# Norm means kept as columns of tokens, and the state-space scan taken in turn with the projections

## The reference

```python
def rms_norm(x, g):
    y = x32 * lax.rsqrt(jnp.mean(x32 * x32, axis=-1, keepdims=True) + RMS_EPS)
    return y * g

# first_block, DEPTH = 2
for l in range(DEPTH):
    u = rms_norm(h, ln_mix[l])
    (aq, ak, av, bq, bk, bv, cq, ck, cv, dq, dzf, dzb, di, dg, gz) = split_in(u @ w_in[l])
    # y_a windowed attention, y_b rope attention, y_c differential attention, y_d gated linear attention
    merged = sum(gate[:, :, n] * (y_n @ w_branch[l, n]))
    h = h + merged @ w_out[l]
    u = rms_norm(h, ln_ffn[l])
    h = h + (silu(u @ w_ffn_gate[l]) * (u @ w_ffn_up[l])) @ w_ffn_down[l]
x = rms_norm(h, ln_final)[:, META_END:]

# second_block: shift, scale and gate come from a conditioning vector
x = x + gate0 * rms_norm(swiglu(modulate(rms_norm(x, pre1), ...)), post1)
h = modulate(rms_norm(x, premix), shift, scale)
q, k, v, u = split(h @ w_in2)                  # 512, 128, 128 and 512 columns
attn = sliding_window_attention(q, k, v, sinks)
ssm = s5_ssm(u, ...)                           # y = Re(C x) + D u, x a diagonal complex recurrence; GELU, GLU
y = concat(rms_norm(attn, n_attn), rms_norm(ssm, n_ssm)) @ w_out2
x = x + gate1 * rms_norm(y, postmix)
x = x + gate2 * rms_norm(swiglu(modulate(rms_norm(x, pre2), ...)), post2)
```

## Time and profile before

| | us |
|---|---|
| median of 3 runs (lowest to highest) | 3252.58 (3252.03 to 3252.73) |
| profiled execution | 3256.16 |
| its span | 3253.3 |
| mean granted TensorE clock over the span | 0.964 of full |

### The profile page before, as it was taken

The page is one execution under the profiler, slowest core; times in us unless marked ns, Lnnn a source line. Parts: engine busy times, 40 slices in busy tenths (PEclk is TensorE's granted clock), DMA queues, the critical chain, the costliest instruction groups (busy, mean ns, idle before and its releaser), DMA issues.

```text
span 3253.3 us, 51837 instructions
## 1 busy us (share of the span) xinstructions
PE 3037.7 (93%) x21724; PEld 2591.9 (80%) x21724; DVE 1775.1 (55%) x3325; ACT 1011.7 (31%) x1740; POOL 220.4 (7%) x455
## 2 busy tenths in 40 slices
PE   7989999999999899999999999989999797789997
PEld 7767998999999887789897888858888364568886
DVE  4564577457556447457745757556356344553334
ACT  4655232232122246523223222242222114332221
POOL 0130221000000101122200000000000000000000
PEclk8999999999999999999999999989999898999999
DMA  5201111135433320112123545212234200113231
GB/s 176 99 15 46 58 59 57 70 131 175 150 134 111 119 78 27 46 50 66 58 71 141 180 146 178 100 53 104 101 126 162 91 34 12 66 65 105 84 103 70
DMA packets 74495, 302.48 MB, mean 93 GB/s; under 512 B 10728, under 2 KB 11112, under 8 KB 69272
## 3 DMA queue, kind: packets, MB, share of 16 engines
q1 hardware_dynamic: 57880, 230.04, 20.8%
q0 software_dynamic: 16384, 69.13, 5.8%
HBM read 288.51 MB, written 14.63 MB: 93 GB/s over the span
## 4 chain that ended last, share of the span: by engine, by line
PE 83%; DVE 9%; ACT 5%; issue 2%; POOL 0%; DMA 0%; DVEq 0%; ACTq 0%; SPq 0%
PE acc L1047 18%; PE acc L1048 17%; PE acc L1049 17%; PE acc L1309 5%; PE acc L1310 5%; PE acc L1311 5%; PE acc L1081 3%; ACT temps L1690 2%; PE acc L1212 2%; DVE work L1999 1%; PE acc L1066 1%; PE acc L1354 1%; PE acc L1186 1%; DVE normed L2017 1%; PE acc L1375 1%
## 5 line engine op out<-in xcount | busy, mean ns | idle before, releaser
L1048 PE MATMUL acc<-normed_r,toep_r 128*128 128x512 f32 (+1 forms) x1824 | 643.7, 353 | 0.0
L1619 ACT ACTIVATE toep_r<-ring 128x1024 fp32r<-128x1024 f32 (+2 forms) x340 | 392.7, 1157 | 711.4 <-PE acc L1049 710.6
L2050 DVE TENSOR_TENSOR ring_r<-ring,toep_r 128x1024 fp32r<-128x1024 f32 (+2 forms) x340 | 458.1, 1348 | 263.6 <-ACT toep_r L1619 263.3
L1048 PEld LDWEIGHTS acc<-normed_r,toep_r 128*128 128x128 f32 x1824 | 345.3, 189 | 46.3 <-issue 0.2
L1047 PE MATMUL acc<-work_r,toep_r 128*128 128x512 f32 (+1 forms) x1024 | 354.7, 346 | 6.5 <-DVE temps_r L2041 6.3
L1049 PE MATMUL acc<-work_r,ring_r 128*128 128x512 f32 (+1 forms) x1024 | 353.6, 345 | 0.0
L1047 PE MATMUL acc<-mixed_r,toep_r 128*128 128x264 f32 (+1 forms) x1056 | 344.1, 326 | 5.1 <-DVE ring_r L2050 4.4
L1049 PE MATMUL acc<-mixed_r,ring_r 128*128 128x264 f32 (+1 forms) x1056 | 340.0, 322 | 0.0
L1047 PE MATMUL acc<-temps_r,toep_r 128*128 128x512 f32 x768 | 304.5, 396 | 24.6 <-DVE normed_r L2036 15.2
L1048 PE MATMUL acc<-work_r,toep_r 128*128 128x512 f32 (+1 forms) x880 | 307.3, 349 | 0.0
L1309 PE MATMUL acc<-residual_r,toep_r 128*128 128x264 f32 (+1 forms) x1024 | 302.1, 295 | 1.6 <-DVE mixed L2237 1.6
(11 more groups left out here) (394 smaller groups left out, 5362.8 us busy)
## 6 DMA issues: line engine op xcount, KB each, us to landing
ring<-in_w_pair SPq DMA_DIRECT2D x176, 512.0 KB, 3.5
ring<-in_w_down SPq DMA_DIRECT2D x64, 704.0 KB, 4.1
ring<-in_w_gb SPq DMA_DIRECT2D x64, 640.0 KB, 3.9
extra<-in_w_ada POOLq DMA_DIRECT2D x18, 1024.0 KB, 6.4
toep<-in_w_ada POOLq DMA_DIRECT2D x18, 1024.0 KB, 5.9
ring<-in_w_tm SPq DMA_DIRECT2D x24, 512.0 KB, 4.5
ring<-in_w_out SPq DMA_DIRECT2D x24, 512.0 KB, 3.5
ring<-in_w_fm SPq DMA_DIRECT2D x20, 512.0 KB, 3.9
```

The costliest lines, as they stand in the source:

```text
L1048: mm(out, wh, xl[:, a:z], start=False, stop=False)
L1619: A(high(ld), slot(ld), ACT.Copy).then_inc(S["w_high"], 1)
L2050: V.tensor_tensor(low(ld), slot(ld), high(ld), ALU.subtract).then_inc(S["w_low"], 1)
```

## The change

The mean stands in columns of tokens. `mean_tile` takes the squares as stationary operand, 128 tokens (or 88, for 528) at a time, and one constant column as moving operand; each matmul leaves 128 tokens' partial sums in one column of bank 6. DVE sums the columns of all tiles (a tensor_reduce), ACT roots 128x4 (or 88x6), DVE inverts as much, and a new `spread_root` on TensorE multiplies each column, broadcast as stationary operand, by the identity, which puts the result of all tokens into all partitions of bank 7 (or 6 and 7). DVE's norm instructions read it from there. In the scaled FFN norms ACT copies it to `RINV`, and the spread stands behind u0. `sqrt_table` is a root of one column, put ahead of places where roots follow, so that the table is loaded there: at the start, ahead of the second half's down jobs of every FFN, ahead of the out jobs of both layers, and ahead of n_attn's squares. An Exp moves behind pre1's squares.

Behind premix ACT adds the shift, tile by tile, and TensorE waits per tile. The u jobs come first (and their loads); q, k and v go one by one, through bank 7, between the scan's parts. Some scratch tiles move to other buffers, since U now stays in use.

```diff
@@ norm(): where the mean and the root stand
-                     acc=PS[:, 6:6 + len(pieces), 0:pieces[0][1] - pieces[0][0]],
+                     rows=88 if len(pieces) == 2 else P, count=6 if len(pieces) == 2 else 4,
+                     r=PS[:, 6:8, 64:328] if len(pieces) == 2 else PS[:, 7:8, :],
@@ TensorE, mean_tile and spread_root
-                for s, (a, z) in enumerate(n["pieces"]):
-                    last = mm(n["acc"][:, s, :], mean[P * len(n["tiles"])], x[:, a:z],
-                              start=i == 0, stop=i == len(n["tiles"]) - 1)
+                a, at = n["pieces"][0][0], n["count"] * (min(i, 1) if n["total"] is not None else i)
+                for t in range(n["count"]):
+                    last = mm(PS[0:n["rows"], 6, at + t:at + t + 1], x[:, a + n["rows"] * t:a + n["rows"] * (t + 1)],
+                              mean[P * len(n["tiles"])][:, 0:1], start=True, stop=True, skip_group_check=True)
                 last.then_inc(S["sq_used"], 1)
+            def spread_root(n):
+                if n["n"]:
+                    wait(pe, norms[n["n"] - 1]["done"][-1])
+                pe.wait_ge(S["mean_inverted"], n["n"] + 1)
+                rows, each_piece = n["rows"], n["count"] // len(n["pieces"])
+                for t in range(n["count"]):
+                    a = rows * (t % each_piece)
+                    last = mm(n["r"][:, t // each_piece, a:a + rows], n["stat"][:, t:t + 1].to_broadcast([rows, P]),
+                              ident[0:rows, 0:rows], start=True, stop=True, skip_group_check=True)
+                last.then_inc(S["mean_spread"], 1)
@@ TensorE, ffn
                         split_lin(u)
+                        if i == 0 and f["scaled"]:
+                            spread_root(f["norm"])
@@ TensorE, second_block (every other norm: spread_root behind its mean_square)
                 mean_square(b2["premix"])
-                wait(pe, b2["premix"]["done"][-1])
-                for j in b2["q"] + b2["k"] + b2["v"] + b2["u"]:
-                    lin(j)
+                spread_root(b2["premix"])
+                for i, j in enumerate(b2["u"]):
+                    lin(j, [(S["u_shifted"], k + 1) for k in range(KT)] if i == 0 else ())
@@ TensorE, state_space (projection(i): the matmuls of q, k or v number i)
                 local_states(0)
+                projection(0)
                 lag_kernels()
+                local_states(1)
+                projection(1)
                 for q in range(4):
-                    if q < 3:
-                        local_states(q + 1)
-                    outputs(q)
+                    if q == 3:
+                        projection(5)
+                    outputs(q)
+                    if q < 2:
+                        local_states(q + 2)
+                    if q < 3:
+                        projection(q + 2)
@@ ACT, root, ffn, second_block
-                A(two(RINV, n["pieces"]), n["acc"], ACT.Sqrt, bias=epsc).then_inc(S["mean_read"], 1)
+                act.wait_ge(S["mean_summed"], n["n"] + 1)
+                A(n["stat"], n["stat"], ACT.Sqrt, bias=epsc[0:n["rows"], :]).then_inc(S["mean_rooted"], 1)
...
                     root(f["norm"])
+                    act.wait_ge(S["mean_spread"], f["norm"]["n"] + 1)
+                    A(two(RINV, f["pieces"]), f["norm"]["r"], ACT.Copy).then_inc(S["rinv_ready"], 1)
...
+                for k in range(KT):
+                    wait(act, b2["premix"]["done"][k])
+                    x = U[:, k, META:L]
+                    A(x, x, ACT.Identity, bias=mod[:, 24 + k:25 + k]).then_inc(S["u_shifted"], 1)
@@ DVE, rinv
-                V.reciprocal(r, r).then_inc(S["rinv_ready"], 1)
+                V.tensor_reduce(n["stat"], PS[0:n["rows"], 6, 0:k * n["count"]].rearrange("p (i t) -> p t i", i=k), AX, ALU.add
+                                ).then_inc(S["mean_summed"], 1)
+                dve.wait_ge(S["mean_rooted"], n["n"] + 1)
+                V.reciprocal(n["stat"], n["stat"]).then_inc(S["mean_inverted"], 1)
```

More of the change, by code:

```diff
@@ L319, in build @@
         ostat = cell(20)
+        meanstat, rootc = [cell(6) for _ in range(2)], cell(1)
         dec = [cell(2) for _ in range(2)]
@@ L428, in build @@
         KD = lambda q, lag: span(X, KD0 + 512 * q + P * lag, P)
-        MP = [span(Ut, 512 * k, 512) for k in range(4)]
-        WS, ZS = pair_of(Ut, 2048), pair_of(Ut, 3072)
+        MP = [span(X, xa + 512 * k, 512) for k in range(4)]
+        WS, ZS = pair_of(toep, 4096), pair_of(X, xa + 2048)
         ZO = [pair_of(E, 1536), pair_of(Yt, 4 * L)]
@@ L670, in build @@
         b2["premix"] = norm(H, b2["post1"]["done"], range(KT), TOKENS)
[L671 to L681, removed]
         b2["u"] = []
@@ L686, in build @@
             j.freed = mark("fm_ready")
+        b2["qkv"] = [load(ins["w_in2"][i], KT, cols=P) for i in range(6)]
+        for i, ld in enumerate(b2["qkv"]):
+            ld.done = (S["proj_full"], i + 1)
         b2["glu"] = []
@@ L1500, in second_block @@
                 mean_square(b2["pre1"])
+                spread_root(b2["pre1"])
                 ffn(b2["ffn1"], ssm=True)
@@ L1515, in second_block @@
                 mean_square(b2["n_attn"])
+                spread_root(b2["n_attn"])
                 mean_square(b2["n_ssm"])
+                spread_root(b2["n_ssm"])
                 for i, j in enumerate(b2["out"]):
@@ L1519, in second_block, with projection @@
                 mean_square(b2["postmix"])
+                spread_root(b2["postmix"])
                 mean_square(b2["pre2"])
+                spread_root(b2["pre2"])
                 ffn(b2["ffn2"])
                 mean_square(b2["post2"])
+                spread_root(b2["post2"])
+            def projection(i):
+                ld = b2["qkv"][i]
+                pe.wait_ge(w_ready[ld.slot], 16 * (ld.turn + 1))
+                if i:
+                    pe.wait_ge(S["proj_read"], i)
+                for t in range(4 if i == 5 else 1):
+                    for k in range(KT):
+                        if i == 5:
+                            a = META + P * t
+                            last = mm(PS[:, 7, P * t:P * t + P], U[:, k, a:a + P], slot(ld)[:, k, :], start=k == 0,
+                                      stop=k == KT - 1)
+                        else:
+                            last = mm(PS[:, 7, :], slot(ld)[:, k, :], U[:, k, META:L], start=k == 0, stop=k == KT - 1)
+                last.then_inc(S["proj_full"], 1)
             def state_space():
@@ L1680, in ffn @@
                         advance(u.loads[0])
+                    if half:
+                        sqrt_table()
                     for i, j in enumerate(f["down"][half]):
@@ L1970, in first_block @@
                     high_weights(j.loads[0])
+                sqrt_table()
                 squares(b2["n_attn"])
-                squares(b2["n_ssm"], b2["n_attn"]["done"][-1])
+                squares(b2["n_ssm"])
                 high_tiles(b2["x_out"])
@@ L2761, in first_block @@
                 added(b2["post1"], fg(1))
-                normed(b2["premix"], fg(2), U, shift(3))
+                normed(b2["premix"], fg(2), U)
                 state_space()
```

71 lines of the change are left out of this document (47 added, 24 removed).

## The result

The changed kernel takes 3261.77 us (median of 14 runs, 3257.66 to 3266.42) against 3254.54 (14 runs, 3252.03 to 3257.94) for the kernel before: ratio 1.002, 95% interval 1.0012 to 1.0028. It is slightly slower, where 3240 was forecast.

A forecast was written before the change was run, and what follows sets the result against it. TensorE's work plus its waits, for norm reciprocals and behind premix, was taken to bound the kernel. Norm gains and losses, +8.0 in the FFN and -20.5 in the scan summed to -12.5: 3240 us, range 3206 to 3251.

The forecast's parts named there:

- The small chain and its norms: In every norm, small sum, root, reciprocal and spread take 1.85 us warm or 2.8 cold; post1 took 5.42 before.
- The half-clock mean tile: In norms at half clock, a mean tile's eight records cost 1.71 us, above the pace at which squares arrive.
- the burst at 578.70: 20 narrow records after idle took 3.75 us, against 2.02 at 325.58; read as narrow matmuls not raising the clock.
- rival (a): Narrow matmuls in the norms run at full clock, mean tiles cost 0.87: -45.2 us, 3207; chance 0.18.
- The FFN norms: In the two scaled FFN norms, silu waits for the spread and an uncovered table load: +4.0 us each.
- The mixer: Premix's first use to first score: per-tile shift, u first, projections inside the scan; 110.9 us against 131.4, -20.5.
- Rival (b): The six projections inside the scan run at half clock: +41.4 us there, 3281 in all; chance 0.06.
- the sum: Terms of the edited places, from norms to scan, added to -12.5 us for the whole kernel.
- the forecast has 0.64: Chance given to the main forecast for the whole kernel, with its own range 3231 to 3246.
- the four norms behind dense work: post1, final, postmix and post2 start at high clock and take 3.3 us for 5.42: -2.1 each, -8.4.
- the prediction's cold start of the projections: At the u jobs behind premix, some 2.2 us lost, half of the 4 us until full pace.
- Rival (c): No change: squares loaded as weights cost up to 0.25 us a record, 2.0 a tile: 3253; chance 0.12.

The follow-up runs named there:

- e5: Changed kernel with wide mean tiles, root and reciprocal back in the two scaled FFN norms, early loads ahead of both layers' out jobs removed; 3247.07 us, ratio 0.9978.
- e2: Changed kernel with all thirteen norms put back to wide and all early table loads removed, keeping the mixer's new order; 3236.21 us, ratio 0.9935.
- e3: Changed kernel with eight norms wide again; columns stay in ly1.norm, final, post1, postmix and post2; 3231.10 us, ratio 0.9922.
- e9: e3's kernel with ly1.norm wide as well, columns left in final, post1, postmix and post2 alone; 3233.64 us, ratio 0.993.
- e7: Changed kernel plus two wide fp32 matmuls, results unused, ahead of the second model's attention; 3252.29 us, ratio 0.9995.
- e12 to e15: Changed kernel plus one, three, four and again two unused wide matmuls ahead of the second model's attention; profiled runs 3260.16, 3251.76, 3256.71, 3255.00 us.
- e15: Repeat of e7, two unused wide matmuls ahead of the second model's attention, for a second profile; profiled run 3255.00 us.
- e5 and e6: Changed kernel with wide norms back: e5 the two scaled FFN norms, 3247.07 us; e6 the six with all squares on TensorE, 3241.34 us.
- e11: Changed kernel plus eight small unused identity matmuls between ly1.norm's mean tiles and its spread; 3261.23 us, ratio 1.0019.
- e1: Changed kernel with the second model's mixer put back to its old order, all norms keeping columns; 3279.99 us, ratio 1.0069.

## Why the prediction was wrong

**What held.** *The small chain and its norms.* Every norm moved the way that was forecast, within 1.2 us each. The half-clock mean tile, the term that I said decides, was forecast at 1.71 and measured at 1.72 in premix (clock 0.50 throughout), and the reading of the burst at 578.70 against the one at 325.58 was right; rival (a), narrow matmuls at full clock, fell. That small matmuls behind an idle stretch leave the clock low was an estimate from that one burst; pre1 and premix now show it, with 64 records in 13.79 and 13.78 us, all at 0.50. *The FFN norms.* +4.0 each was forecast, +4.0 and +3.6 came, and e5 takes them away. *The mixer.* -19.0 forecast from premix to the first score, -19.0 measured, and e2 alone gives -20.4. Rival (b), half clock in the projections, fell: 1.00 over the whole scan (2623 to 2690).

**The step that failed is the sum.** It adds the edited places and takes the rest of the kernel as it was. In "the forecast has 0.64" and its range there is no term for stages without an edit. But TensorE's sparse stages, the attentions of both layers and of the second model, run in part at half clock, and for how long is not fixed: in layer 0 such stretches summed to 58 us in the profile before and to 65 in the changed kernel's (counted as for layer 1), in layer 1 to 27 and 44, and in the second model's attention to 24 us where the first score stood 105.0 us behind the clock's last rise (e2, e3, e9), and to 48 where it stood 105.6 behind it. In this kernel the three stages took +2.8, +5.0 and +6.8, 14.6 us together, of which 6.8 with 48 us at half clock in place of 24, and 5.0 with 44 in place of 27. The 2.8 of layer 0 comes and goes between executions of the same code, and is a term of the range that was missing rather than a cost of the change. The rest of the error, 4.9, is in sizes: the four norms behind dense work +2.5 together, since their spreads took 2.04 or 2.05 at half clock (0.50) in final, postmix and post2 (only post1's met the full clock, 1.13 at 1.00); ly1.norm +0.7; n_attn and n_ssm +0.6; and small amounts elsewhere. The 4 us in the prediction's cold start of the projections are 4.7 by its own two times; in the changed kernel the clock rose 3.2 us behind their first matmul (2581.11).

**Rival (c) was nearer to the measured time, by a wrong way.** It had 3253 from a record of 0.25 instead of 0.213. The record was 0.215, and the loss came from elsewhere.

**What e7 and e12 to e15 show, and what they don't.** That moving the start of the second model's attention changes the length is shown: 41, 27, 10, 20, 20 us for five kernels that differ by 0.86 us steps, each repeated one the same. These runs also add work, but e5 and e6 (31 us) and e2, e3 and e9 (14 us) do not, and there too the length goes with the distance from the clock's last rise. So that the stretch was long in the changed kernel because of where its start lay is shown for this stage: two wide matmuls more take 9.5 us away, and the mixer with other norms leaves 14 us. For the layers it is argued only: e9 shows that ly1.norm's columns are not the cause, and e11 moved the sum from 44 to 41. Fourteen of the fifteen profiles of kernels with columns in some norm have 41 or 44 us in layer 1 and add 4.1 to 6.1 us of lag there; e15 has 34 and adds 2.7, with the same code as e7, which has 44 and adds 5.0. The kernel before and e2, which have no columns, have 27, and e2 adds nothing. That holds for e9 too, which has columns only in norms that come after both layers, but the early table loads in all FFNs. So what lengthens them stays open. By what rule the clock comes back is not settled.

**The two parts of the change.** The mixer's order is worth -20.4 (e2), the columns +23.4 (e1), and part of that is half clock in stages that neither touches. Columns pay in norms with a sum behind dense work (e3 against e2: -5.1 for five of them), and cost in norms of four or eight tiles and in the scaled FFN norms (in the table +1.2 for ly0.norm, +2.6 for pre1, +1.9 for pre2, +6.0 for n_attn and n_ssm, +4.0 and +3.6 in the FFN). The changed kernel pays for the good with the bad, and e3, which keeps the one and leaves the other, is 25.5 us faster than the kernel before.

The table load of 1.28 was all that a switch cost here: in n_attn's stretch of the changed kernel the load and the root that needed it follow each other without a gap:

```profile
2771.51 1.99 ACT L1671 ACTIVATE toep_r<-ring 128x1024 fp32r<-128x1024 f32 x2
2773.52 1.28 ACT L1649 ACT_TABLE_LOAD   x1
2774.82 0.20 ACT L1649 ACTIVATE small<-small 128x1 f32<-128x1 f32 x1
```

No gap stands ahead of the load either: the two copies before it ended at 2773.50, and it started at 2773.52.

## What to carry to other kernels

Replacing a wide matmul by many of one column saves columns and not weight loads: a mean tile had two records with a load each and has eight now, and PEld is busy for 4.00 of 4.00 us in premix, where it was busy for 1.54 and 0.89 of 4.00. Behind 2.38 us of idle TensorE, premix's 64 one-column records ran at a clock of 0.50, though TensorE was busy for all of their 13.78 us, and a tile took 1.72, against 1.13 for post1's wide one at full clock. Here such a chain paid behind dense work, with few such tiles on the path (-5.1 for five norms), and I would take it only there. Where a kernel has sparse TensorE stages, put their half-clock time into the range of every forecast, with both signs, for any change that moves their start; here it was worth 9.5 us in one stage, more than most single edits, and in layer 0 some 5 us between executions of the same code. And when a change moves the time little, take the lag of the same instructions in the two traces, stage by stage: it shows in one table that -28 and +35 are hidden in +7.

## What the runs showed of the hardware that was not expected

- Two extra wide matmuls, 1.7 us of work, made the kernel 9.5 us faster (3261.77 to 3252.29), by a half-clock stretch of 10 us in place of 41.
- The length of that stretch is the same in two profiles of one kernel (41 and 41, 10 and 10), and goes with the distance from the clock's last rise to the stage's first matmul: 31 us at 104.2 and 104.5, 14 at 105.0 (three kernels), 41 at 105.6 (three kernels, four profiles), 27 at 106.7, 10 at 107.5, 20 at 108.4 and 109.2.
- In layer 0 ten profiles of the same instructions differ by 5.3 us (-1.8 to +3.5 of lag).
- The 14 times of the changed kernel stand at three levels, near 3258, 3262 and 3266, with mean clocks of 0.955, 0.953 to 0.954, and 0.953.
- Through 13.78 us of one-column matmuls in premix, with TensorE busy for all of them (2562.68 to 2576.46), the granted clock stayed at 0.50.
- The spread's eight records took 1.05 (at 1786.67) and 1.13 (at 2559.18) at a clock of 1.00, and 2.04 or 2.05 at 0.50.
